# A first projection block from tokens that are only scaled, with the shift added per channel afterwards

## The reference

```
modulation = silu(c) @ w_ada + b_ada          # 12 blocks of 512 for layer 0: shift = 0,1; scale = 2,3; others later
h    = rmsnorm(x, norm_mix) * (1 + scale) + shift
proj = h @ w_in                               # z | xbc (1536 wide) | dt | hy
xbc  = silu(depthwise_conv5(xbc))             # then the SSD scan, the Hyena part, and so on
```

## Time and profile before

| what | us |
|---|---|
| median of three runs | 1284.57 (1284.48 to 1286.18) |
| span of the profiled execution | 1282.6 |
| TensorE busy in it | 1204.8 (94%) |
| VectorE, ScalarE, POOL busy | 458.2, 325.3, 231.2 |
| first projection matmul starts | 27.68 |
| second projection block done | 78.32 |

### The profile page before, as it was taken

How to read it: one execution, slowest core, us unless ns; L and a number is a source line. 1 busy time by engine, 2 the same in 40 slices (tenths; PEclk the granted TensorE clock), 3 DMA queues, 4 the chain that set the end, 5 groups by cost and what they waited for, 6 DMA issues and landing times.

```text
span 1282.6 us, 16879 instructions
## 1 busy us (share of the span) xinstructions
PE 1204.8 (94%) x6504; PEld 678.7 (53%) x6504; DVE 458.2 (36%) x963; ACT 325.3 (25%) x831; POOL 231.2 (18%) x281
## 2 busy tenths in 40 slices
PE   6999999999999999999999878999999989999786
PEld 4455654555455554466555443755555575555442
DVE  1452088643237850162111112323374251111115
ACT  4313374301022300141111112414353331111113
POOL 1000053200033511011212111444010011212102
PEclk9999999999999999999999999999999999999998
DMA  9997910675940109439999998962330879999995
GB/s 341 359 387 262 367 60 1 224 270 200 375 131 1 66 10 416 142 136 406 419 419 419 419 420 355 369 97 39 139 111 1 334 280 420 418 420 420 421 420 207
DMA packets 94516, 343.15 MB, mean 268 GB/s; under 512 B 12734, under 2 KB 16532, under 8 KB 69617
## 3 DMA queue, kind: packets, MB, share of 16 engines
q1 hardware_dynamic: 73680, 309.47, 61.4%
q0 software_dynamic: 13872, 25.78, 7.4%
q10 hardware_dynamic: 6897, 6.97, 1.6%
HBM read 340.35 MB, written 28.43 MB: 288 GB/s over the span
## 4 chain that ended last, share of the span: by engine, by line
PE 74%; DMA 15%; DVE 5%; POOL 3%; ACT 2%; issue 2%; SPq 0%; DVEq 0%; ACTq 0%; POOLq 0%
PE bank L927 65%; DMA arena<-in_moe_w_down_dram 5%; PE bank L931 5%; DMA ring<-in_moe_w_down_dram 4%; DMA ring<-in_moe_w_up_dram 3%; PE bank L958 3%; DMA ring<-in_w_ada_dram 2%; PE bank L1706 1%; POOL ring L2905 1%; POOL hT L2908 1%; DVE arena L2727 1%; POOL arena L2908 1%; DMA arena<-in_hy_freq_dram 0%; PE bank L1012 0%; DVE arena L2724 0%
## 5 line engine op out<-in xcount | busy, mean ns | idle before, releaser
L927 PE MATMUL bank<-ring,arena 128*64 128x256 f32 (+3 forms) x2592 | 422.5, 429 | 34.5 <-DMA ring<-in_moe_w_up_dram 12.0
L927 PEld LDWEIGHTS bank<-ring,arena 128*64 128x64 f32 (+1 forms) x2592 | 212.8, 143 | 215.4 <-issue 109.5
L927 PE MATMUL bank<-hT,ring 128*128 128x384 f32 (+2 forms) x928 | 293.7, 472 | 1.0 <-DVE hT L2260 0.7
L927 PEld LDWEIGHTS bank<-hT,ring 128*128 128x128 f32 x928 | 170.4, 190 | 119.1 <-issue 16.2
L927 PE MATMUL bank<-arena 128*64 128x256 f32 (+7 forms) x858 | 130.9, 396 | 7.6 <-DMA arena<-in_moe_w_down_dram 1.7
L2683 DVE TENSOR_TENSOR hT<-hT,bank 128x256 f32<-128x256 f32 x32 | 13.5, 420 | 242.1 <-ACT hT L2047 242.1
L927 PEld LDWEIGHTS bank<-arena 128*64 128x64 f32 (+3 forms) x858 | 62.3, 143 | 58.9 <-issue 38.0
L2047 ACT ACTIVATE hT<-bank 128x256 f32<-128x256 f32 x32 | 12.3, 384 | 230.8 <-PE bank L927 230.8
L931 PEld LDWEIGHTS bank<-cst,hT 128*128 128x128 f32 x368 | 46.7, 190 | 38.2 <-issue 34.3
L2688 DVE COPY arena<-bank 128x512 f32<-128x512 f32 x32 | 22.1, 691 | 121.3 <-PE bank L927 101.5
L927 PE MATMUL bank<-ring,hT 128*128 128x512 f32 x144 | 63.0, 593 | 0.0
(11 more groups left out here) (338 smaller groups left out, 1224.2 us busy)
## 6 DMA issues: line engine op xcount, KB each, us to landing
ring<-in_moe_w_up_dram SPq DMA_DIRECT2D x28, 2048.0 KB, 20.5
ring<-in_moe_w_down_dram SPq DMA_DIRECT2D x26, 2048.0 KB, 19.4
ring<-in_w_ada_dram SPq DMA_DIRECT2D x24, 2048.0 KB, 15.5
ring<-in_moe_w_gate_dram SPq DMA_DIRECT2D x24, 2048.0 KB, 21.7
ring<-in_ev_w_in_dram SPq DMA_DIRECT2D x10, 2048.0 KB, 12.8
arena<-in_moe_w_gate_dram SPq DMA_DIRECT2D x8, 2048.0 KB, 13.4
arena<-in_moe_w_down_dram SPq DMA_DIRECT2D x6, 2048.0 KB, 22.1
ring<-in_ev_w_out_dram SPq DMA_DIRECT2D x4, 2048.0 KB, 16.2
```

Of the source, the lines that this page charges most:

```text
L927: return nc.tensor.matmul(out, lhsT, rhs, start=start, stop=stop_, skip_group_check=True)
```

## The change

1. **Order of loads.** The scale block ada 2 comes first, in two halves with a semaphore each; then the first half of xbc 0, ada 3, the second half, and only then the shift blocks ada 0 and 1, and xbc 1. Ada 4 to 9 are computed behind chunks 7 and 11.
2. **Scaled tokens only.** The chunks go to a new tile `hS` = x * gain, without the shift. The four chunks of xbc 0 are projected from `hS`. When the shift is known, VectorE adds it to `hS` and so writes `hT`, with which all later chunks are projected.
3. **The shift's part.** TensorE multiplies the shift (`shc`) with weight block xbc 0 (`shift_products`), ScalarE copies, TensorE sums (`shs`), and the result `shb`, one number per channel and group, is the bias of ScalarE's copy of chunks 0 to 3. The last eighth of these chunks' products stands inside chunk 4.
4. **Sums** are made for each modulation block by itself (`first_sums`, two columns) instead of one set for a pair (four columns).
5. **Small loads.** ScalarE issues five loads, the first 256 columns of the constants among them, all on `cond_in`. The rest of the constants and ten parameter loads (`rows_in`, 16 * `N_ROWS_IN`) are issued by POOL after it has waited for `first_x_in`. VectorE waits for `rows_in` before it writes `d8`. The parameters' transposes are one bank's filling behind the first half of the projection.
6. **Norm.** ScalarE squares one half of each token tile, VectorE the other; each tile has its own semaphore. Heating is 10 matmuls. The table for silu is loaded earlier.

Elsewhere some semaphores are merged (`results_out`, `zeroed`, `fin`), with the same waits.

```diff
-ADA_AFTER = {("xbc", 3): (0, 4), ("xbc", 7): (0, 6), ("xbc", 11): (0, 8), ("z", 3): (0, 10),
+ADA_AFTER = {("xbc", 7): (0, 4), ("xbc", 11): (0, 6, 8), ("z", 3): (0, 10),
...
-    first = [("ada", 0, 0), ("ada", 0, 2)]
-    for kind in [("xbc",)] * 3 + [("z",)] * 2 + [("hy", q) for q in range(3) for _ in range(2)]:
+    first = [("ada", 0, 2), ("xbc", 0), ("ada", 0, 3), ("ada", 0, 0), ("ada", 0, 1)]
+    for kind in [("xbc",)] * 2 + [("z",)] * 2 + [("hy", q) for q in range(3) for _ in range(2)]:
...
+        hS = area(0, KD, T)
+        shc, shb = area(14400, KD, 32), area(14656, 2 * SHIFT_LATER)
+        dsq = area(3072, NT, 512)
...
-                if k == first_k:
+                if k == 0:
+                    for h in range(2):
+                        sp.dma_start(block_view(LOADS[k])[:, 4 * h:4 * h + 4, :], block_source(LOADS[k])[:, 4 * h:4 * h + 4, :])\
+                            .then_inc(S("full%d" % k if h else "first_ada_in"), 16)
+                elif k == first_k:
...
+                if b == 2:
+                    pe.wait_ge(S("first_ada_in"), 16)
+                else:
+                    arrived(("ada", 0, b))
                 w = block_view(("ada", 0, b))
                 for k in range(KD):
                     q = k % 4
...
+                    if b == 2 and k == 4:
...
+            def shift_products():
+                ps = open_bank("shw")
+                pe.wait_ge(S("shifted"), 3)
+                w = block_view(("xbc", 0))
+                for k in range(KD):
+                    q = k % 4
+                    last = nc.tensor.matmul(ps[32 * q:32 * q + 32, :], shc[:, k, :], w[:, k, :], start=k < 4, stop=k >= 4,
+                                            tile_position=(0, 32 * q), skip_group_check=True)
+                last.then_inc(done, 1)
+
+            pe.wait_ge(S("cond_in"), 16 * 5)
             ps = open_bank("cond")
-            tr(ps[:, 0:2 * KD], prow[0:2 * KD, 0, :]).then_inc(done, 1)
-            heat(open_bank("warm0"), 12).then_inc(done, 1)
-            pe.wait_ge(S("rows_in"), 16 * (sum(len(t) for t in ROWS) - 2))
-            for i in range(4):
-                ps = open_bank("par", i)
-                tr(ps[:, 0:NROWS[i]], prow[0:NROWS[i], i, :]).then_inc(done, 1)
-            ps = open_bank("par", 4)
-            pe.wait_ge(S("d8"), 1)
-            tr(ps[:, 0:KD], d8[0:KD, :]).then_inc(done, 1)
+            tr(ps[:, 0:4 * KD], prow[0:4 * KD, 0, :]).then_inc(done, 1)
+            heat(open_bank("warm0"), 10).then_inc(done, 1)
+            ps = open_bank("par", 1)
+            tr(ps[:, 0:NROWS[1]], prow[0:NROWS[1], 1, :]).then_inc(done, 1)
+            first_scaled(0, 0)
+            first_scaled(1, 0)
             pe.wait_ge(S("silc"), 1)
-            first_ada_block(0, 0)
-            for t in range(NT):
-                first_scaled(t, 0)
-            first_ada_block(2, 1)
+            first_ada(2)
+            first_scaled(2, 0)
+            first_scaled(0, 1)
             pe.wait_ge(S("small_in"), 16 * 2)
-            first_ada_sums(0)
-            for t in range(NT):
-                first_scaled(t, 1)
+            first_sums(2)
+            first_scaled(1, 1)
+            first_scaled(2, 1)
             pe.wait_ge(S("first_x_in"), 16)
-            for c in range(4):
-                took(pe, *PLAN[PRIOR[JOB[("xbc", c)]]][0])
-                if c < 3:
-                    first_x(c, 0)
-                    if c:
-                        first_ada_block(2 * c - 1, c - 1)
+            first_x(0, range(4))
+            first_x(1, range(4))
+            first_ada(3)
+            first_x(2, range(4))
+            first_sums(3)
+            first_x(3, range(4))
+            parameters()
+            arrived(("xbc", 0))
+            first_x(0, range(4, 7))
+            first_ada(0)
+            first_x(1, range(4, 7))
+            first_sums(0)
+            first_ada(1)
+            first_x(2, range(4, 7))
+            first_sums(1)
+            first_x(3, range(4, 7))
+            shift_products()
+            arrived(("xbc", 1))
+            pe.wait_ge(S("shifted"), 4)
+            for c in range(SHIFT_LATER, KX):
+                if c == SHIFT_LATER:
+                    w = block_view(("xbc", 1))
+                    took(pe, *PLAN[PRIOR[JOB[("xbc", c)]]][0])
+                    for k in range(KD):
+                        if k == 4:
+                            row_sums(("shs",), ("shw",))
+                            for x in range(SHIFT_LATER):
+                                open_bank("xbc", x)
+                                first_x(x, (KD - 1,)).then_inc(done, 1)
+                            open_bank("xbc", c)
+                        last = mm(bank("xbc", c)[:, 0:T], w[:, k, 0:P], hT[:, k, :], k == 0, k == KD - 1)
+                    last.then_inc(done, 1)
                 else:
-                    first_x(c, 0, range(2))
-                    first_ada_sums(1)
-                    first_x(c, 0, range(2, 4))
-            arrived(("xbc", 0))
-            for c in range(4):
-                open_bank("xbc", c)
-                first_x(c, 1).then_inc(done, 1)
-                ada_after("xbc", c)
-            for c in range(4, KX):
-                if c % 4 == 0:
-                    arrived(("xbc", c // 4))
-                project(("xbc", c), block_view(("xbc", c // 4)), c % 4 * P, hT)
+                    if c % 4 == 0:
+                        arrived(("xbc", c // 4))
+                    project(("xbc", c), block_view(("xbc", c // 4)), c % 4 * P, hT)
...
+            for i, name, at, n in ((0, "c_ctx", 0, 8), (0, "c", 8, 8), (0, "norm_mix", 16, 16), (1, "b_ada", 0, 96)):
+                act.dma_start(prow[at:at + n, i, :], param_rows(name)).then_inc(S("cond_in"), 16)
+                if at == 8:
+                    act.dma_start(cst[:, 0:2 * P], K["k_cst"][:, 0:2 * P]).then_inc(S("cond_in"), 16)
...
+            def first_squares(t):
+
+                A_(unread, xR[:, t, 0:512], ACT.Square, scale=D ** -0.5, accum_out=nsum[:, t, 0:1]).then_inc(S("xsq"), 1)
+                squared[0] += 1
+                act.wait_ge(S("xsq"), squared[0])
+                act.wait_ge(S("xsq1"), t + 1)
+                A_(nrs[:, t:t + 1], nsum[:, t, 0:1], ACT.Sqrt, bias=nsum[:, t, 1:2]).then_inc(S("xrt"), 1)
...
-                    A_(hT[:, k, cols(t)], bank("xn", "mix0", t, g)[:, cols(c)], ACT.Identity, scale=gmod[:, 0, k, v:v + 1],
-                       bias=mod[:, 0, k, v:v + 1]).then_inc(S("act_first"), 1)
+                    A_(hS[:, k, cols(t)], bank("xn", "mix0", t, g)[:, cols(c)], ACT.Copy, scale=gmod[:, 0, k, v:v + 1])\
+                        .then_inc(S("act_first"), 1)
...
+                    if c < SHIFT_LATER:
+                        A_(cpad[:, c % 2, PAD:PAD + LP], ps[:, 0:LP], ACT.Identity, bias=shb[:, 2 * c:2 * c + 1])
+                        A_(cpad[:, c % 2, 2 * PAD + LP:2 * PAD + T], ps[:, LP:T], ACT.Identity, bias=shb[:, 2 * c + 1:2 * c + 2])\
+                            .then_inc(taken["act"], 1)
...
-            dve.wait_ge(S("d2_in"), 16)
+            nc.vector.memset(conds[0], 0.0).then_inc(S("const"), 1)
+            nc.vector.memset(shc, 0.0)
+            nc.vector.memset(cpad, 0.0)
+
+            def first_squares(t):
+                dve.wait_ge(S("x_in%d" % t), 16)
+                nc.vector.tensor_tensor_reduce(out=dsq[:, t, :], in0=xR[:, t, 512:D], in1=xR[:, t, 512:D], scale=1.0 / D, scalar=EPS,
+                                               op0=mult, op1=add, accum_out=nsum[:, t, 1:2]).then_inc(S("xsq1"), 1)
+
+            first_squares(0)
+            for t in range(NT):
+                if t + 1 < NT:
+                    first_squares(t + 1)
+                root("mix0", t)
+            dve.wait_ge(S("rows_in"), 16 * N_ROWS_IN)
             COPY(d8[0:KD, :].rearrange("c (h r) -> c h r", h=2), over(d2[0:KD, :], HDIM)).then_inc(S("d8"), 1)
-            dve.wait_ge(S("cst_in"), 16)
-            for t in range(NT):
-                root("mix0", t)
-            took(dve, "par", 3)
...
+            took(dve, "par", 1)
+
+            def first_mod(b):
+                full(dve, "ada", 0, b)
+                at = PAR["b_ada"] + 4 * b
+                take(TT(mod[:, 0, 4 * b:4 * b + 4, :], bank("ada", 0, b)[:, 0:8].rearrange("p (m v) -> p m v", m=4),
+                        over(par[:, at:at + 4], 2), add))
+                took(dve, "ada", 0, b)
+
+            for g in range(2):
+                first_mod(g + 2)
                 ks = slice(4 * g, 4 * g + 4)
                 gains = STT(out=gmod[:, 0, ks, :], in0=mod[:, 0, 8 + 4 * g:12 + 4 * g, :], scalar=1.0,
                             in1=over(par[:, PAR["norm_mix"] + 4 * g:PAR["norm_mix"] + 4 * g + 4], 2), op0=add, op1=mult)
                 gains.then_inc(S("first_gain"), 1)
                 dve.wait_ge(S("first_gain"), g + 1)
-
-            for g in range(2):
-                first_mod(g)
                 full(dve, "xn", "mix0", 1, g)
                 for c, t in FIRST_MOD["dve"]:
```

(44 more changed lines are left out.)

170 lines of the change are left out of this document (85 added, 85 removed).

## The result

| | before | after |
|---|---|---|
| median, 4 runs each | 1285.03 us | 1294.94 us (1292.62 to 1295.64) |
| ratio of the runs | | 1.0076, 95% interval 1.0064 to 1.0089 |
| span of the profiled execution | 1282.6 | 1293.8 |
| first projection matmul | 27.68 | 28.69 |
| second projection block and blocks ada 4, 5 done | 78.32 | 89.42 |

The change makes the kernel 0.8% slower: 9.9 us between the medians, 11.2 between the two spans. (The profiled execution is the slowest of the four.) The range of 1293 to 1302 held the time; the forecast of 1298.2 was 3.3 us too high. The time alone does not single the forecast out: two rivals had named 1294.2 and 1295.7, which lie nearer.

A forecast was written before the change was run, and what follows sets the result against it. TensorE, busy 1204.8 of 1282.6 us, was taken to bound the kernel. Later start 3.3, added work 7.8 and clock 2.5 sum to 13.6, giving a 1296.2 span; 2.0 more for the median gives 1298.2, range 1293 to 1302.

The forecast's parts named there:

- The deciding step: Before first modulation, VectorE waits for all ten POOL-issued parameter loads, so the projection starts at 31.0, not 27.68.
- The start's term: First projection matmul moves from 27.68 to 31.0 behind the parameter rows, costing 3.3 us.
- the lower bound: Earliest projection start with the rows' wait, 28.1: weight half at 15.5, 5.5 of issues, 5.3 of landing, 1.8 after.
- The added work: TensorE work new or moved in between first projection matmul and end of second projection block: 7.8 us.
- The clock: TensorE, empty from about 20 to 31, drops to 1.2 GHz; early matmuls at half pace cost 2.5 us.
- The pass-through: Whatever moves TensorE's early work moves the kernel's end by as much; nothing found that later waits for something else.
- The rival with a start at 27.0: Small rows land sooner, projection starts at 27.0, clock still lost: 9.6 us more, 1294.2; chance 0.12.
- The rival without the clock's drop: VectorE's wait binds but TensorE's clock stays up: 11.1 us more, 1295.7; chance 0.13.
- The not-slower rival: VectorE's wait never ends last, projection starts at 21.0, no idle stretch: +1.1 us, 1285.7; chance 0.05.

The follow-up runs named there:

- doubling: The kernel with the late wait, with the shift's products with the weight block and their sums done twice: 1288.67 us, ratio 1.0041.
- two pairs of traces: Changed kernel beside itself with 15 more heating matmuls before the first projection matmul, two sets; with heating 1293.52 us, ratio 1.0070, and 1292.88 us, ratio 1.0074.
- the kernel with the late wait: Changed kernel with VectorE's wait for the parameter rows and its copy of d8 moved behind both halves' scaled chunks: 1285.33 us, ratio 1.0014.
- the front alone: Kernel before plus small loads, halved squares, 10 heating matmuls, moved parameter transposes and VectorE's late rows wait, without the shift's changes: 1283.20 us, ratio 0.9993.
- the rows unheld: Changed kernel with POOL's ten parameter loads issued ahead of its wait for the first weight half: 1285.39 us, ratio 1.0013.

## Why the prediction was right, step by step

- **The deciding step** held: VectorE's wait for `rows_in` ended last, released by the last parameter load, and TensorE stood behind it. Either way of removing it brings the start to 22.1 to 22.3 and the time from 1.0076 to 1.0014 and 1.0013. The forecast for a start without the wait was about 21; measured 22.1. TensorE began at 9.15, when b_ada had landed, not at about 7, and made good 1.0 of these 2.1 us on the way.
- **The start's term** was mis-sized: 3.3 forecast, 1.0 measured (28.69 for 31.0). All pieces but one came in under their estimates: the weight half at 16.8 (17.7), the nine row issues ahead of the last one 4.58 (4.95), the last one's landing 5.08 (6.0), and from there to the first matmul 1.4 (1.8); only POOL's way from the weight half to the first row issue was longer, 0.8 (0.6). The landing missed as much as the weight half. Its 6.0 came from three loads of another kind, the step weights and two small ones next to them, and those took 6.7, 6.0 and 5.8 again in the changed kernel, while the nine rows of parameters took 4.8 to 5.1. Even the 5.3 of the lower bound, which stands in no row, was above the 5.08. The fixed figure of about 2.0 us per POOL load that the Trainium skill gives (DMA: Bandwidth & Descriptors, "Anatomy of one DMA — SWDGE (gpsimd) path") errs the other way here: the last row load, 30 KB, took 5.0 to 5.9 us in all twelve traces with it on POOL.
- **The added work**: 7.8 forecast. Measured from the ninth projection matmul on: 89.42 - 37.02 = 52.40 for 78.32 - 33.08 = 45.24, so 7.2. The parts that a run priced: shift's products and their sums 2.6 by doubling (3.05 in the sum, of which 0.2 is a change back that doubling does not add), one set of sums with the bank's wait 1.46, with a change back saved (1.35 without it). The parameters' transposes took 0.51 for 0.8. Block 0 and the other set of sums were priced by no run of their own.
- **The clock**: 2.5 forecast, 2.9 measured, in two pairs of traces (8.32 and 8.27 us with the drop, 5.39 and 5.38 without). The idle stretch was 6.7 us, not the 10 or 11 forecast, and the level was lost all the same. The Trainium skill (TensorE: Matmul & The Clock Gate, "HAM oscillation — how this bites in real kernels") says that a wait between bursts of matmuls puts the array back to the lower level; the windows 24:26 agree, with 0.69 and then 0.50. That all 2.9 reach the end is shown at the block and fits the spans of both pairs; the medians do not show it.
- **The pass-through** held: 11.1 us at 89.42, 11.2 at the end of the span, so no slack of a later stage shows. That the two agree to 0.1 is in part luck, since the stretch behind the block differs by up to 2.5 us among the other traces, and once by more.
- Sum: 1.0 + 2.9 + 7.2 = 11.1 for 13.6 forecast. Of the 3.3 us between 1298.2 and 1294.94 this is 2.4; the other 0.9 is the distance from the profiled span to the median, taken as 2.0 and measured as 1.1. The rival with a start at 27.0 was 9.6; the measured start, 28.69, lies between it and the forecast, a little nearer to the rival. The rival without the clock's drop named 11.1, the very sum that was measured, but by luck: the drop is in the windows, and its 2.9 stand where the start's term was 2.3 too large and the added work 0.6.
- **The not-slower rival** was rightly held small: the rows landed at 27.3, not before 19.2. But its price, +1.1, was close to what the kernel without the wait does: +1.6 at the block, +0.14% in time.

## What to carry to other kernels

Moving loads off a busy queue moves their landing, and their bytes then stand before another block; look on every engine for who waits for them, and in what order that engine's own program stands. A wait for something that nobody needs yet costs as much as the next thing in line behind it. And count what an algebraic split adds to the engine that bounds the kernel: in the kernel with the late wait the projection starts 5.6 us earlier and 7.2 us more stand behind its start. Of the 5.6, the front alone gives 3.0 without any split; the split and its order of loads give the other 2.6, for most of the 7.2. The single parts of the front (small loads, halved squares, less heating) were not measured apart, and no version is shown to be faster than the kernel before.

## What the runs showed of the hardware

- The last parameter load (30 KB, issued by POOL) took 5.0 to 5.1 us to land beside saturated transfers, whether issued at 7.19 or at 22.19; in the two traces with TensorE heating it took 5.78 and 5.93.
- The 64 KB of step weights, read in 64-byte pieces, go with a dip of the DMA rate shortly before they land: 207 GB/s in 9:10 before, 184 in 29:30 in the changed kernel, 130 in 24:25 with the rows unheld. In 9:10 the last two ran at 393 and 386.
- TensorE, idle from 21.95, lost the higher level within 24:25 and had it back inside 34:35 after working from 28.69, at a cost of 2.9 us.
